# K, Q, Z and V of four heads at a time as rows of tokens, with 512 weight columns moving

## What is computed

```python
kv = einsum('bsd,de->bse', rmsnorm(x, kv_norm), w_kv)      # K and V of three groups: 2048 x 12288
qz = einsum('bsd,de->bse', rmsnorm(x, b_norm), b_w_in)     # Q of three groups and Z: 2048 x 8192
s  = einsum('nbqhd,nbkhd->nbhqk', q, k) * HEAD_DIM ** -0.5 + bias    # then a softmax in each group
o  = sum over groups of alpha * softmax(s) v                # alpha from the groups' log-sum-exps
x  = x + einsum('bse,ed->bsd', o * silu(z), b_w_out)
out = rmsnorm(x, final_norm)
```

## Time and profile before

| | before |
|---|---|
| median of 3 runs | 1415.42 us (1415.39 to 1417.6) |
| the profiled execution's own time | 1417.62 us |
| its span, first to last instruction | 1415.8 us |
| PE busy | 1403.5 us, 99% of the span, 8344 matmuls |
| DVE, ACT, POOL busy | 887.3, 690.6, 375.0 us |
| DMA | 286.91 MB, 203 GB/s over the span |

### The profile page before, as it was taken

The page is one execution under the profiler, slowest core; times in us unless marked ns, Lnnn a source line. Parts: engine busy times, 40 slices in busy tenths (PEclk is TensorE's granted clock), DMA queues, the critical chain, the costliest instruction groups (busy, mean ns, idle before and its releaser), DMA issues.

```text
span 1415.8 us, 22981 instructions
## 1 busy us (share of the span) xinstructions
PE 1403.5 (99%) x8344; PEld 1243.0 (88%) x8344; DVE 887.3 (63%) x1495; ACT 690.6 (49%) x1023; POOL 375.0 (26%) x165
## 2 busy tenths in 40 slices
PE   9999999999999999999999999999999999999997
PEld 8999999988888888888888888888888888888786
DVE  6999999632544444455676666676666676666423
ACT  5444444675644444444454444454444354444443
POOL 2988888888400000000000000000000000001595
PEclk9999999999999999999999999999999999999999
DMA  9866666555667566589787787788787788775562
GB/s 251 232 181 186 196 184 185 187 184 188 224 215 245 191 232 230 187 236 234 184 230 204 187 210 184 193 231 209 183 214 184 184 231 218 182 213 178 219 208 89
DMA packets 420829, 286.91 MB, mean 203 GB/s; under 512 B 10667, under 2 KB 374779, under 8 KB 420396
## 3 DMA queue, kind: packets, MB, share of 16 engines
q1 hardware_dynamic: 420300, 285.35, 70.0%
q10 hardware_dynamic: 480, 0.90, 0.2%
HBM read 267.79 MB, written 10.55 MB: 197 GB/s over the span
## 4 chain that ended last, share of the span: by engine, by line
issue 76%; POOL 17%; PE 6%; DVE 1%; POOLq 0%; ACT 0%; DVEq 0%
POOL w_lo L402 16%; PE bank L481 2%; PE bank L483 2%; PE bank L482 2%; PE bank L1530 0%; DVE x_hat_mem L1071 0%; PE bank L1534 0%; PE bank L1517 0%; POOLq L401 0%; PE bank L1538 0%; DVE mem_a L1076 0%; DVE resid L1457 0%; DVE w_lo L402 0%; ACT w_hi L747 0%; ACT y L1045 0%
## 5 line engine op out<-in xcount | busy, mean ns | idle before, releaser
L402 POOL TENSOR_TENSOR w_lo<-raw,w_hi 128x1024 fp32r<-128x1024 f32 x155 | 373.1, 2423 | 1025.3 <-ACT w_hi L393 999.4
L393 ACT ACTIVATE w_hi<-raw 128x1024 fp32r<-128x1024 f32 x248 | 261.7, 1060 | 318.6 <-PE bank L483 192.5
L431 DVE TENSOR_TENSOR w_lo<-raw,w_hi 128x1024 fp32r<-128x1024 f32 x224 | 266.7, 1219 | 62.0 <-ACT w_hi L425 60.8
L425 ACT ACTIVATE w_hi<-raw 128x1024 fp32r<-128x1024 f32 x224 | 232.7, 1053 | 126.3 <-PE bank L457 118.0
L461 PE MATMUL bank<-mem_a,w_hi 128*128 128x256 f32 x736 | 206.6, 281 | 0.7 <-DVE mem_a L1076 0.7
L462 PE MATMUL bank<-mem_a,w_hi 128*128 128x256 f32 x736 | 205.5, 279 | 0.0
L463 PE MATMUL bank<-mem_a,w_lo 128*128 128x256 f32 x736 | 204.5, 278 | 0.0
L402 DVE TENSOR_TENSOR w_lo<-raw,w_hi 128x1024 fp32r<-128x1024 f32 x97 | 118.9, 1226 | 135.0 <-ACT w_hi L393 134.9
L457 PE MATMUL bank<-mem_b,w_hi 128*128 128x512 f32 x512 | 202.5, 396 | 0.0
L453 PE MATMUL bank<-mem_b,w_hi 128*128 128x512 f32 x512 | 202.3, 395 | 0.0
L481 PE MATMUL bank<-w_hi,mem_a 128*128 128x512 f32 x504 | 197.2, 391 | 1.9 <-POOL w_lo L402 1.9
(11 more groups left out here) (211 smaller groups left out, 2123.6 us busy)
## 6 DMA issues: line engine op xcount, KB each, us to landing
raw<-b_w_in_dram SPq DMA_DIRECT2D x128, 512.0 KB, 5.7
raw<-w_kv_dram SPq DMA_DIRECT2D x48, 1024.0 KB, 6.8
raw<-w_kv_dram SPq DMA_DIRECT2D x96, 512.0 KB, 5.6
raw<-a_w_in_dram SPq DMA_DIRECT2D x45, 1024.0 KB, 5.8
raw<-a_w_out_dram SPq DMA_DIRECT2D x16, 1024.0 KB, 5.1
raw<-b_w_out_dram SPq DMA_DIRECT2D x16, 1024.0 KB, 5.2
prob<-prob_sq SPq DMA_DIRECT2D x240, 32.0 KB, 1.9
v_dram<-v_stage SPq DMA_DIRECT2D x12, 512.0 KB, 3.4
```

The source lines that it names most:

```text
L393: nc.scalar.activation(w_hi[:, stream.half_slot(half), :], raw[:, slot, part:part + HALF], ACT.Copy).then_inc(hi_done, 1)
L402: eng.tensor_tensor(w_lo[:, stream.half_slot(half), :], raw[:, slot, part:part + HALF], w_hi[:, stream.half_slot(half), :].bitcast(F32), A ...
L425: nc.scalar.activation(w_hi[:, QKV.half_slot(half), :], raw_half(half), ACT.Copy).then_inc(hi_done, 1)
L431: nc.vector.tensor_tensor(w_lo[:, QKV.half_slot(half), :], raw_half(half), w_hi[:, QKV.half_slot(half), :].bitcast(F32), ALU.subtract).the ...
```

## The change

V, K, Q and Z are no longer two stages. Four heads at a time, a quad, PE makes 10 chunks of 512 columns: three of K, three of Q, one of Z, three of V (`QUAD_CHUNKS`), each in 4 slabs, all with tokens stationary and 512 weight columns moving (`project_slab`, `wide_products`). The 7 chunks of K, Q and Z are evicted as rows of tokens by ACT (`evict`), turned in squares of 32 x 32 by DVE (`turn_chunk`), and stored by SP in `kqz_dram` in runs of 64 elements (256 bytes; `store_chunk`). Z comes back into `y2` by 16 DMAs per quad issued by SP (`load_z`), K and Q of each head by 4 DMAs issued by POOL into one of two buffers (`load_kq`). V goes to `v_dram` as before. The loop over heads is gone; all programs are written out slab by slab, and `SCORES_AFTER` says after which slab the scores of each head are made. The attend of head h - 1 stands just ahead of the scores of head h.

The moves of squares of the probabilities go from SP to POOL, all but those of head 14. The half slots of `w_hi` and `w_lo` are 5 instead of 7, and all W slabs use all 5. In the output projection DVE and POOL share the low parts of the first 8 slabs, and the last four heads are attended inside it. The additions of half banks and the two scalings by rows are gone (the scale by token is now in the eviction).

```diff
-RAW_SLABS, HALF_SLOTS, SLAB_HALVES, HEAD_RING = 4, 7, 4, 7
+RAW_SLABS, HALF_SLOTS, SLAB_HALVES = 4, 5, 4
...
+QUAD = 4
+QUADS = HEADS // QUAD
+QUAD_CHUNKS = (("k", 0), ("k", 1), ("k", 2), ("q", 0), ("q", 1), ("q", 2), ("z", 0), ("v", 0), ("v", 1), ("v", 2))
+PER_QUAD = len(QUAD_CHUNKS)
...
+W_CHUNKS = QUADS * PER_QUAD
...
+END_ORDER = ((0, 0), (0, 1), (0, 2), (1, 0), (1, 1), (1, 2), (0, 3), (1, 3),
+             (2, 0), (2, 1), (2, 2), (2, 3), (3, 0), (3, 1), (3, 2), (3, 3))
+ALL_SLABS = W_SLABS + len(END_ORDER)
...
+SCORES_AFTER = (36, 46, 54, 62, 76, 86, 94, 102, 116, 126, 134, 142, 150, 153, 156, 158)
+LATE = HEADS - QUAD
...
+def w_slot(half):
+    return (half + 1) % HALF_SLOTS
...
+def kq_slot(h):
+    if h % QUAD == 0:
+        return PER_QUAD * SLABS * (h // QUAD) + 31
+    return SCORES_AFTER[h - 1] + (4 if h > LATE else 5) - (h == HEADS - 1)
...
+        kqz_dram = nc.dram_tensor("kqz_dram", [P, HEADS, SQUARES, TURNED, TT * SQUARE], F32, kind="Internal")
...
+        def load_wide(sp, s, src):
+            if s < RAW_SLABS:
+                sp.wait_ge(lo_pool, W_LO_POOL - 2 * RAW_SLABS + 2 * s + 2)
+            else:
+                for half in (2 * (s - RAW_SLABS), 2 * (s - RAW_SLABS) + 1):
+                    wait_lo(sp, half)
+            sp.dma_start(raw[:, s % RAW_SLABS, :], src).then_inc(raw_in[s % RAW_SLABS], 16)
+        def wide_hi(act, s):
+            act.wait_ge(raw_in[s % RAW_SLABS], 16 * (W_BASE // RAW_SLABS + s // RAW_SLABS + 1))
+            for half in (2 * s, 2 * s + 1):
+                if half != SLAB_HALVES:
+                    act.wait_ge(mm_done, w_used(half - (SLAB_HALVES if half < SLAB_HALVES else HALF_SLOTS)))
+                part = (half % 2) * HALF
+                nc.scalar.activation(w_hi[:, w_slot(half), :], raw[:, s % RAW_SLABS, part:part + HALF],
+                                     ACT.Copy).then_inc(hi_done, 1)
...
+        def project_slab(pe, s, q, banks, operand, ready=None):
+            for half in (2 * s, 2 * s + 1):
+                wait_lo(pe, half)
+                for k in range(RKT // 2):
+                    kt = q * RKT + (half % 2) * (RKT // 2) + k
+                    if ready is not None:
+                        pe.wait_ge(ready, kt + 1)
+                    for t in range(TT):
+                        mm = wide_products(half, kt, k, t, banks[t][:, :], operand)
+                mm.then_inc(mm_done, 1)
...
+        def move_squares(eng, h, done):
+            eng.wait_ge(squares_turned, TT * (h + 1))
+            row = BLOCKS * SQUARE
+            for i in range(SQUARES):
+                for j in range(SQUARES):
+                    eng.dma_start(prob_of(h)[j * SQUARE:(j + 1) * SQUARE, :, i * row:(i + 1) * row],
+                                  prob_sq[i * SQUARE:(i + 1) * SQUARE, :, j * row:(j + 1) * row]
+                                  ).then_inc(done, 16)
...
+            def store_chunk(c):
+                n, (which, g) = c // PER_QUAD, kind_of(c)
+                if which == "v":
+                    sp.wait_ge(evicted, TT * (c + 1))
+                    sp.dma_start(v_dram.ap()[:, g, :, n * CHUNK:(n + 1) * CHUNK], staged(c)).then_inc(v_stored, 16)
+                    return
+                sp.wait_ge(sq_turned, TT * (squares_before(c) + 1))
+                sp.dma_start(kqz_dram.ap()[:, QUAD * n:QUAD * (n + 1), :, c % PER_QUAD, :].rearrange("p h j s -> p (h j) s"),
+                             sq_stage[:, :].rearrange("p (n s) -> p n s", s=TT * SQUARE)).then_inc(sq_stored, 16)
+            def load_z(n):
+                sp.wait_ge(sq_stored, 16 * TURNED * (n + 1))
+                if n == 0:
+                    sp.wait_ge(resid_stored, 16)
+                for h in range(QUAD * n, QUAD * (n + 1)):
+                    for j in range(SQUARES):
+                        sp.dma_start(y2[j * SQUARE:(j + 1) * SQUARE, h, :].rearrange("b (i s) -> b i s", i=SQUARES),
+                                     kqz_dram.ap()[:, h, j, TURNED - 1, :].rearrange("(i b) s -> b i s", i=SQUARES)
+                                     ).then_inc(z_loaded, 16)
...
+            for s in range(ALL_SLABS):
+                if s < W_SLABS:
+                    load_wide(sp, s, wide_slab(*divmod(s, SLABS)))
+                else:
+                    load_wide(sp, s, out_slab(b_w_out[0], *END_ORDER[s - W_SLABS]))
...
-            def move_squares(h):
...
-                sp.wait_ge(squares_turned, TT * (h + 1))
-                for i in range(SQUARES):
-                    for j in range(SQUARES):
-                        row = BLOCKS * SQUARE
-                        sp.dma_start(prob[j * SQUARE:(j + 1) * SQUARE, :, i * row:(i + 1) * row],
-                                     prob_sq[i * SQUARE:(i + 1) * SQUARE, :, j * row:(j + 1) * row]
-                                     ).then_inc(prob_turned, 16)
...
-            with sp.Fori(PEELED, HEADS) as h:
-                col = sp.snap(h * P)
-                cols = [sp.snap(col + (2 * j if j < NG else j - NG) * D) for j in range(HEAD_SLABS)]
...
+                if s % SLABS == 2 and s >= 10 and kind_of((s - 10) // SLABS)[0] == "v" and (s - 10) // SLABS < W_CHUNKS - 1:
+                    store_chunk((s - 10) // SLABS)
+                if s % SLABS == 3 and 11 <= s < W_SLABS and kind_of((s - 11) // SLABS)[0] != "v":
+                    store_chunk((s - 11) // SLABS)
+                if s % (PER_QUAD * SLABS) == 36 and s < W_SLABS:
+                    load_z(s // (PER_QUAD * SLABS))
...
+            def load_kq(h):
+                pool.wait_ge(sq_stored, 16 * (TURNED * (h // QUAD) + TURNED - 1))
+                positive(pool, scores_done, h - 1)
+                for j in range(SQUARES):
+                    pool.dma_start(kq[h % 2][j * SQUARE:(j + 1) * SQUARE, :, :],
+                                   kqz_dram.ap()[:, h, j, 0:TURNED - 1, :].rearrange("(i b) w s -> b i (w s)", i=SQUARES)
+                                   ).then_inc(kq_loaded[h % 2], 16)
+            for n in range(2):
+                load_kq(n)
+            for first in range(0, HEADS, QUAD):
+                load_kq(first + 2)
+                move_squares(pool, first, prob_turned)
+                load_kq(first + 3)
+                move_squares(pool, first + 1, prob_turned)
+                if first == LATE:
+                    continue
+                move_squares(pool, first + 2, prob_turned)
+                load_kq(first + 4)
+                load_kq(first + 5)
+                move_squares(pool, first + 3, prob_turned)
...
+            def evict(c):
+                act.wait_ge(mm_done, w_used(2 * SLABS * (c + 1) - 1))
                 if c == 0:
                     act.wait_ge(v_scale_ready, 1)
-                if c >= 2:
-                    act.wait_ge(v_stored, 16 * (c - 1))
+                if c >= 2 and kind_of(c - 2)[0] == "v":
+                    act.wait_ge(v_stored, 16 * (values_before(c - 2) + 1))
+                elif c >= 2:
+                    act.wait_ge(sq_turned, TT * (squares_before(c - 2) + 1))
                 for t in range(TT):
+                    scale = {"k": v_scale, "v": v_scale, "z": rstd}.get(kind_of(c)[0])
                     nc.scalar.activation(staged(c)[:, t, :], bank[2 * (c % 2) + t][:, :], ACT.Copy,
...
             def head_hi(h):
...
+                act.wait_ge(kq_loaded[h % 2], 16 * SQUARES * (h // 2 + 1))
+                positive(act, scores_done, h)
+                nc.scalar.activation(in_tiles(k_hi[:, :]), kq_tokens(h, 0), ACT.Copy).then_inc(k_his, 1)
+                nc.scalar.activation(in_tiles(q_hi[:, :]), kq_tokens(h, NG), ACT.Copy).then_inc(q_his, 1)
+                for g in range(1, NG):
+                    nc.scalar.activation(in_tiles(q_t[:, g - 1, :]), kq_tokens(h, NG + g), ACT.Copy).then_inc(q_copied, 1)
             def tanh_gate(h):
-                act.wait_ge(kz_copied, (h + 1) * (NG + 1))
-                nc.scalar.activation(z_tanh[:, :], z_t[:, :], ACT.Tanh, scale=0.5).then_inc(z_tanh_ready, 1)
...
+                act.wait_ge(z_loaded, 16 * SQUARES * QUAD * (h // QUAD + 1))
+                positive(act, z_gate_ready, h)
+                nc.scalar.activation(z_tanh[:, :], y2[:, h, :], ACT.Tanh, scale=0.5).then_inc(z_tanh_ready, 1)
...
-            with act.Fori(PEELED, HEADS) as h:
-                for j in range(HEAD_SLABS):
-                    head_step(h, PEELED, j)
...
+                if s % SLABS == 2 and 0 <= (s - 6) // SLABS < W_CHUNKS:
+                    evict((s - 6) // SLABS)
+                for h in range(HEADS):
+                    if s == kq_slot(h):
+                        head_hi(h)
+                    if s == SCORES_AFTER[h] + 4:
+                        tanh_gate(h)
+                    if s == SCORES_AFTER[h] + 5:
+                        exps(h)
+                    if h < LATE and s == SCORES_AFTER[h] + 9:
+                        values_hi(h)
+                        probs_hi(h)
...
+            def turn_chunk(c):
```

(43 more changed lines are left out.)

792 lines of the change are left out of this document (349 added, 443 removed).

## The result

The changed kernel takes 1420.18 us (median of 10 runs, 1417.06 to 1421.9) against 1415.36 us: a ratio of 1.0029, with a 95% interval of 1.0019 to 1.0038. It is slower, as forecast, but by 5 us and not by 20. The profiled execution has a span of 1418.6 us, 1.8 us under its own time of 1420.43.

A forecast was written before the change was run, and what follows sets the result against it. PE's matmul time was taken as the bound; 1415.8 - 15.2 - 0.5 + 2 x 9.2 + 6.3 + 6.4 + 4.4 gave a 1435.6 us span, forecast 1435 us, range about 1402 to 1463.

The forecast's parts named there:

- The places: PE waits near 780 and 1010 us, near 1250 for the attend, soon after for Q; nothing between.
- PE's saving: Projection of K, Q and Z: 28 chunks at 609.3 us replace 624.5, saving 15.2, plus 0.5 for four small matmuls.
- The deciding place: End of a quad's sixth K or Q chunk: POOL's moves for heads 3, 7, 11 stand behind 8 loads; 9.2, 9.2, 6.3 us.
- the next wait, for Z: Last quad, scores of head 13: Z's store and 16 loads come late after head 11's restart; PE waits 6.4 us.
- the tail: B_OUT: POOL makes low parts behind 32 moves and a load; PE waits 4.4 us.
- What c is: POOL's time to issue one DMA in the heads, taken as 0.95 us, between 0.645 and 1.28.
- The recorded sign of being wrong: POOL's issue under 0.71 us; further signs: L708's store landing over 8 us after issue, or PE waiting elsewhere.
- POOL issues about as fast as SP: Rival on POOL's queue: c under 0.75 us, 1411 us at 0.645, 1400 at 0.40 or less; chance 0.36.
- 24c - 13.6: PE's wait in us at heads 3 and 7, with 24 POOL issues of c each; 9.2 at c of 0.95.
- Late stores: Rival: stores in 256-byte runs land in 8.4 us instead of 6.0, giving 1445 us, or 1459 at twice 6.0; chance 0.10.
- DVE or ACT as the bound: Rival where transposes, softmax and low parts meet: 1405 us beside a fast POOL, 1440 beside a slow one; chance 0.04.
- POOL at 1.28: Rival: POOL issues at twice SP's pace, lengthening three places and the tail, 1462 us; chance 0.09.

The follow-up runs named there:

- the moves first: Changed kernel with POOL's moves of heads 3, 7 and 11 ahead of the next quad's two loads; 1400.4 us, 0.9892 of the kernel before.
- B_OUT eased: Kernel with POOL's moves ahead of its loads, plus all low parts of B_OUT's first 8 slabs by DVE; 1398.63 us, 0.9876 of the kernel before.
- both: Changed kernel with K and Q loads of heads 4, 5, 8, 9, 12, 13 on SP and B_OUT's first 8 slabs' low parts on DVE; 1398.35 us.
- another run: Changed kernel with K and Q loads of heads 8, 9, 12 and 13 carrying a sixth of their bytes; one run, span 1409.5 us.

## Why the prediction was right and wrong

**The places: right; the direction: right by luck.** PE's saving is as worked out: L510 starts at 399.43 and again at 578.95, 792 matmuls later, 0.2267 us each, as in the earlier trace rows. With the moves first and B_OUT eased the span is 1397.0, and 1396.2 with both: 1400.1, the sum before any wait, less the 1.9 us wait of B_OUT in the earlier trace rows and the 1.9 us by which the slow matmuls behind it were longer. The deciding place, the queue order behind it and the next wait, for Z, are as forecast. The size of the wait for Z (6.4 forecast, 5.28 idle) is near because two links offset each other: SP goes on 9.4 us after the issue of the store of Z instead of 6, and the 16 loads take 8.34 us instead of 10.3. The direction owes to errors that cancel. With the measured c and every other term as it stood, the prediction's own formulas give about 1405 us, faster than before (an estimate: 1400.1, 2.7 for Z and 1.9 for the tail).

**The step that failed: "What c is".** POOL issues a move in 0.53 us and a load in 0.55, not in 0.95, and the three terms that were built on it, 9.2, 9.2 and 6.3 us, measured 3.28, 2.83 and 1.56. 0.95 was the middle of SP's 0.645 and twice that. POOL is faster than SP with the same move, and its slowness in arithmetic, from which the upper value came, says nothing of issuing. The measured value lies between the two rows of SP that the trace had, 0.384 for a plain store and 0.645 for a move. The recorded sign of being wrong, an issue under 0.71, is met; the second, a landing of the store over 8 us, is met by some of the stores (6.7 to 9.6, median 7.3) but not by the three for which POOL waits. The two figures of the Trainium skill ("DMA: Bandwidth & Descriptors", Latency and other measured facts) that stood beside c, 600 ns and 1 us, are times to the first byte, not times that an issue takes: SP's 0.645 does not bear out the one, nor does POOL's 0.53 speak against the other. The rival "POOL issues about as fast as SP" (0.36) held for the pace, but not for the time: its own numbers give 1400 to 1411.

**Why it is not 1405.** With c at 0.53 the formula gives 24c - 13.6, under nothing. Two more terms were too small: POOL goes on 1.4 us later behind the store than taken, and the last move lands 3.3 us later. 3.4 for a store was read where no load was in flight, and 1.9 for a move on SP's queue; on POOL's a move takes over 4 us even with nothing ahead, and here 1.5 MB stand ahead. With these the formula gives 3.9 us for head 3; the trace has 3.28. A smaller c and longer landings half cancel. The span is 17 us off: 18 too much in the idle time, 7 too much in the tail, and 8 that the clock took and the sum did not have.

**What was missing: the clock behind a wait.** The sum counts a wait by its length. The four places cost 7.9 us beside their 13.0 of idle time, nearly all by the clock. The kernel before has one such stretch, behind the 1.89 us of its B_OUT, where its window from 1320 to 1340 us shows a granted clock of 0.91; the prediction did not look there, and the slices of the earlier trace rows are too coarse to show it.

**The tail** was priced at +4.4 us. It came out as -2.4: 1418.6 less 1400.1, 13.0 and 7.9. The old wait of 1.9 us and the 1.9 behind it were gone, and PE waits 0.8 in B_OUT instead.

**The rivals.** Late stores: right in part, since the landing is 7.3 in place of 6.0 (the rival had 8.4), wrong in cause, since runs of 4 KB land after 7.2; the Trainium skill's rule on transfers under 512 bytes ("DMA: Bandwidth & Descriptors", Specifications) does not show in this store. DVE or ACT as the bound: neither, outside of the two ops that POOL held up in B_OUT. POOL at 1.28: no.

## What to carry to other kernels

A wait of the bounding engine can cost more than its length: in the changed kernel 2.8 and 3.3 us of idle time cost 4.8 and 6.3, and in another run 3.24 us at the same place cost 3.55. So a forecast gives such a wait a range, and the loss is read from the granted clock and from the distance between matmuls. A queue whose instructions wait for different things is read for what stands behind each wait, and for the bytes that stand ahead as well as for the issues. A landing time taken from a row holds for the queue of that row and for what was in flight there: a store took 3.4 us with nothing in flight and 7 behind a load, a move 1.9 us on SP's queue and over 4 on POOL's. A change that is 0.3% slower can be the order of three lines away from 1.1% faster; ask which wait ends last, before the change is given up.

## What the runs showed that was not expected

- Of a POOL queue: 0.53 to 0.55 us an issue, faster than SP with the same move (0.60 to 0.65), and landings from 1.9 to 9.0 us for 32 KB in the changed kernel. With nothing of POOL's ahead the median is still 4.5 at head 3, against 1.9 on SP's queue.
- DVE's scaling of 128x512 takes 0.48 us and 2.6 us where it meets a subtraction of POOL, and its own subtraction 1.22 and 2.58. The Trainium skill ("SBUF — State Buffer", SBUF: two separate sides) has the two engines take one pair of ports in turn, for a whole instruction; the rows agree.
- Behind each wait of PE over 3.25 us, and behind some shorter ones, PE works for some microseconds at 1.2 GHz, 0.43 us a matmul of 512 columns, and is back at 0.2267 then; the loss is 1.6 to 3.2 us and does not grow with the wait. Behind 3.24 us at head 3 of one run it did not come at all.
